# Routing a hybrid layer's last token group inside the mixer, with expert slot tables summed per group

## What is computed

```
mix = hybrid_mixer(x, ...)                      # x @ w_in, mLSTM heads | gated short convolution, @ w_out
x   = layer_norm(ALPHA * x + mix, ln_mix_g, ln_mix_b)              # called x1 here
ffn = grouped_moe(x, router_w, router_b, w_gate, w_up, w_down)
out = layer_norm(ALPHA * x + ffn, ln_moe_g, ln_moe_b)

probs = softmax(xf @ router_w + router_b)       # 16 experts in 4 groups of 4
grp   = argmax(sum of the top 2 of each group)  # one expert group per token
the top 2 experts inside it, gates = their probabilities / their sum
y[token] += gate * (silu(x @ w_gate[e]) * (x @ w_up[e])) @ w_down[e]
```

## Time and profile before

| | |
|---|---|
| median of 3 runs (lowest, highest) | 1700.78 us (1699.57, 1702.06) |
| the profiled execution's own time | 1698.55 us |
| span of its profile | 1696.2 us (2.35 us lie around it) |
| mean granted clock of PE | 0.977 of full speed |
| busy: PE, DVE, ACT, POOL | 1611.2, 1086.9, 659.3, 341.4 us |

### The profile page before, as it was taken

How to read it: one execution, slowest core, us unless ns; L and a number is a source line. 1 busy time by engine, 2 the same in 40 slices (tenths; PEclk the granted TensorE clock), 3 DMA queues, 4 the chain that set the end, 5 groups by cost and what they waited for, 6 DMA issues and landing times. The chain is left out here.

```text
span 1696.2 us, 25177 instructions
## 1 busy us (share of the span) xinstructions
PE 1611.2 (95%) x9494; PEld 1395.9 (82%) x9494; DVE 1086.9 (64%) x1799; ACT 659.3 (39%) x919; POOL 341.4 (20%) x275
## 2 busy tenths in 40 slices
PE   7999999999999999999999279999999999999994
PEld 6888888888888888888888269999999999999993
DVE  3536867557676468665585756565676667666777
ACT  3224424143342343341433324443555455545551
POOL 1100015100052000250000012222333323233333
PEclk9999999999999999999999679999999999999997
DMA  7332336322434225253223626666777777777762
GB/s 238 125 100 75 125 125 215 92 91 92 157 138 162 75 75 184 93 197 100 75 100 125 260 68 206 205 208 202 230 243 244 223 234 251 249 228 234 245 210 95
DMA packets 118922, 279.48 MB, mean 165 GB/s; under 512 B 14688, under 2 KB 16864, under 8 KB 118288
## 3 DMA queue, kind: packets, MB, share of 16 engines
q1 hardware_dynamic: 91536, 188.68, 32.8%
q0 software_dynamic: 26688, 87.05, 17.3%
q10 hardware_dynamic: 576, 2.10, 0.3%
HBM read 232.80 MB, written 48.40 MB: 166 GB/s over the span
## 5 line engine op out<-in xcount | busy, mean ns | idle before, releaser
L1056 PE MATMUL mix_acc<-mix_xT_high,mix_w_high 128*128 128x512 f32 x640 | 256.2, 400 | 2.2 <-DVE mix_w_low L793 2.2
L793 DVE TENSOR_TENSOR mix_w_low<-mix_w_raw,mix_w_high 128x2048 fp32r<-128x2048 f32 x73 | 168.7, 2311 | 138.4 <-ACT mix_w_high L648 138.3
L1058 PE MATMUL mix_acc<-mix_xT_high,mix_w_low 128*128 128x512 f32 x640 | 250.7, 392 | 0.0
L1057 PE MATMUL mix_acc<-mix_xT_low,mix_w_high 128*128 128x512 f32 x640 | 249.9, 390 | 0.0
L648 ACT ACTIVATE mix_w_high<-mix_w_raw 128x2048 fp32r<-128x2048 f32 x73 | 139.8, 1915 | 237.8 <-PE mix_acc L1058 223.9
L1799 DVE TENSOR_TENSOR moe_gate_up_low<-kept_w_gate_up_raw,moe_gate_up_high 128x2048 fp32r<-128x2048 f32 x64 | 146.6, 2291 | 80.4 <-ACT moe_gate_up_high L1669 80.4
L2141 PE MATMUL moe_gate_psum<-moe_xT_high,moe_gate_up_high 128*128 128x288 f32 x512 | 154.1, 301 | 1.4 <-DVE moe_xT_low L1816 1.4
L2143 PE MATMUL moe_up_psum<-moe_xT_high,moe_gate_up_low 128*128 128x288 f32 x512 | 152.0, 297 | 0.0
L2142 PE MATMUL moe_gate_psum<-moe_xT_low,moe_gate_up_high 128*128 128x288 f32 x512 | 151.7, 296 | 0.0
L2142 PE MATMUL moe_up_psum<-moe_xT_low,moe_gate_up_high 128*128 128x288 f32 x512 | 151.6, 296 | 0.0
L2141 PE MATMUL moe_up_psum<-moe_xT_high,moe_gate_up_high 128*128 128x288 f32 x512 | 151.5, 296 | 0.0
(11 more groups left out here) (456 smaller groups left out, 3496.2 us busy)
## 6 DMA issues: line engine op xcount, KB each, us to landing
mix_w_raw<-in_w_in SPq DMA_DIRECT2D x57, 1024.0 KB, 5.3
kept_w_gate_up_raw<-in_w_gate SPq DMA_DIRECT2D x32, 1024.0 KB
kept_w_gate_up_raw<-in_w_up SPq DMA_DIRECT2D x32, 1024.0 KB
kept_w_down_raw<-in_w_down SPq DMA_DIRECT2D x32, 1024.0 KB, 8.6
mix_w_raw<-in_w_out SPq DMA_DIRECT2D x16, 1024.0 KB, 5.1
mix_x_rows<-in_x POOLq DMA_DIRECT2D x16, 512.0 KB, 4.6
kept_conv_or_residual<-in_x POOLq DMA_DIRECT2D x16, 512.0 KB, 5.4
x<-kept_conv_or_residual POOLq DMA_DIRECT2D x12, 512.0 KB, 3.3
```

The costliest lines, as they stand in the source:

```text
L793: dve.tensor_tensor(wl[:, stage % 2], raw[:, stage % 2], wh[:, stage % 2].bitcast(F32), ALU.subtract).then_inc(split_l, 1)
L1056: pe.matmul(out, ah, bh, start=first, stop=False)
L1057: pe.matmul(out, ah, bl, start=False, stop=False)
L1058: return pe.matmul(out, al, bh, start=False, stop=last)
```

## The change

Group 3 is written out too, without the X steps, the load and the split for a next group. In its stage 17 DVE takes, normalises and scales row by row; PE turns row 0 between tiles 2 and 3 and the other rows after the last tile. The rows are turned before the bias is added; the bias's part of the logits is a product of `router_w` with a bias column loaded at the start (`late_b`). SP issues the loads of expert 0 after the last stage's load (their buffers now share room with x's and the queries' and keys' tiles, which are done by then). The block `route` is gone; its constants move to POOL's and DVE's work at the start.

Each routed group's share of the slot table is formed in stages 6 to 8 of the next group (`slot_one_hots`, `slot_sums`, `slots_added`), and that of group 3 at the start of the experts. The table is a sum in SBUF; its one-hots are fp32r, 144 columns of three parts. The number of rounds is worked out after `tables` and loaded at the end of the round. ACT splits three parts of expert 0 ahead; DVE's first split moves behind `tables`. B's result of `down` goes to `pg[1]`, `pu[1]`, so that `down(B)` waits for no reader of A; `gate_up`'s step f = 1 waits for the readers of B instead.

```diff
+def slot_one_hots(dve, keep, w, own, turn, n):
+    N, C = 2 * RT, COLS * N_EXPERTS
+    own.step(dve.tensor_copy(w.rank, keep.pair_rank[:, bass.ds(n * N, N)]))
...
+    own.step(dve.tensor_tensor(w.parts[:, :, 2], keep.icol[:].unsqueeze(1).to_broadcast([P, N, C]),
+                               w.col.unsqueeze(2).to_broadcast([P, N, C]), ALU.is_equal))
+    own.step(dve.tensor_tensor(w.place_oh, keep.i128[:].unsqueeze(1).to_broadcast([P, N, P]),
+                               w.place.unsqueeze(2).to_broadcast([P, N, P]), ALU.is_equal))
+    own.wait(turn)
+    for part, by in ((0, w.token), (1, w.high[:].bitcast(F32))):
+        own.step(dve.tensor_tensor(w.parts[:, :, part], w.parts[:, :, 2].bitcast(F32),
+                                   by.unsqueeze(2).to_broadcast([P, N, C]), ALU.mult))
+    own.wait(turn)
+    dve.tensor_tensor(w.parts[:, :, 2], w.parts[:, :, 2].bitcast(F32), w.low.unsqueeze(2).to_broadcast([P, N, C]),
+                      ALU.mult).then_inc(keep.oh_done, 1)
+
+def slot_sums(pe, keep, w, out):
+    for k in range(2 * RT):
+        ins = pe.matmul(out, w.place_oh[:, k], w.parts[:, k].rearrange("p a b -> p (a b)"), start=(k == 0),
+                        stop=(k == 2 * RT - 1))
+    ins.then_inc(keep.s_ps, 1)
+
+def slots_added(dve, keep, ps, own, turn):
+    own.step(dve.tensor_tensor(slots, slots, ps[:, 0:2 * C], ALU.add))
+    own.wait(turn)
+    dve.tensor_tensor(keep.slots[:, 1], keep.slots[:, 1], ps[:, 2 * C:3 * C], ALU.add).then_inc(keep.s_added, 1)
...
@@ mixer, sync @@
+            sp.dma_start(keep.bias_col[:], column(ln_b), allow_slow_non_contiguous=True).then_inc(consts_in, 16)
...
+            sp.wait_ge(acc_full, (NG - 1) * FULL + OUT0 * NT)
+            load_gate_up(sp, keep, w_gate[0], w_up[0])
...
+            load_down(sp, keep, w_down[0])
+            for t in range(NT):
+                sp.wait_ge(v.x1_ready, (NG - 1) * NT + t + 1)
...
+                sp.dma_start(x1_dram[row:row + P], R[:, t]).then_inc(keep.late_x1, 16)
@@ mixer, scalar, last group @@
+                    for t in range(NT):
+                        one = slice(t, t + 1)
+                        act.wait_ge(lvar_done, g + t + 1)
...
+                        if t == NT - 1:
+                            for half in range(2):
+                                turned_rows(act, v_last, g, 1, half)
+                        act.wait_ge(ln_gained, g * NT + t + 1)
+                        act.activation(R[:, t], R[:, t], ACT.Copy, scale=lrs[:, one]).then_inc(ln_done, 1)
+                        if t == NT - 2:
+                            for half in range(2):
+                                turned_rows(act, v_last, g, 0, half)
+                    logits_taken(act, v_last, g, 0, keep.late_b, False)
+                    turned_rows(act, v_last, g, NT - 1, 0)
+                    logits_taken(act, v_last, g, 1, keep.late_b, False)
+                    exponentials(act, v_last, g)
...
@@ mixer, vector @@
+                        for t in range(NT):
+                            take(g, stage, range(t, t + 1))
...
+                            dve.bn_aggr(lmv[:, t], lstat[:, t]).then_inc(lvar_done, 1)
+                            dve.wait_ge(lvar_done, g + t + 1)
+                            dve.scalar_tensor_tensor(out=R[:, t], in0=R[:, t], scalar=lmv[:, t, 0:1], in1=lng[:],
+                                                     op0=ALU.subtract, op1=ALU.mult).then_inc(ln_gained, 1)
...
+                        for half in range(2):
+                            turned_half(NT - 2, half)
+                        add_bias(0)
+                        turned_half(NT - 1, 1)
+                        add_bias(1)
+                        add_bias(2)
+                        centred_logits(dve, keep, v_last, own, g, g)
+                        add_bias(3)
+                        choices(dve, keep, v_last, own, g, g)
+                        ranks(dve, keep, v_last, own, g, g)
...
                     if routed and stage == 6:
                         ranks(dve, keep, v, own, g, g - 1)
-                        kept_of(dve, keep, v, g - 1)
+                        kept_of(dve, keep, v, own, g, g - 1, dve_idle)
+                        slot_one_hots(dve, keep, w, own, g, g - 1)
+                    if routed and stage == 8:
+                        dve.wait_ge(keep.s_ps, g)
+                        slots_added(dve, keep, aux[0][:, 256:256 + 3 * COLS * N_EXPERTS], own, g)
@@ mixer, tensor @@
-                        if (stage, t) in SLOT:
+                        if (stage, t) in SLOT and not (last and stage > LAST_Y):
                             extra(g, *SLOT[(stage, t)])
+                        if routed and (stage, t) == (7, 0):
+                            pe.wait_ge(keep.oh_done, g)
+                            slot_sums(pe, keep, w, aux[0][:, 256:256 + 3 * COLS * N_EXPERTS])
+                        if last and (stage, t) == (6, 0):
+                            for c in range(KC):
+                                ins = pe.matmul(aux[2][0:TW, 0:1], keep.router_w[:, c], keep.bias_col[:, c:c + 1],
+                                                start=(c == 0), stop=(c == KC - 1))
...
+                        if last and (stage, t) == (ST - 1, NT - 2):
+                            turn_rows(pe, keep, v_last, g, 0, R[:, 0], ln_done)
...
+            turn_rows(pe, keep, v_last, g, 1, R[:, 1], ln_done)
+            turn_rows(pe, keep, v_last, g, 2, R[:, 2], ln_done)
...
+            logits(pe, keep, v_last, 0)
+            turn_rows(pe, keep, v_last, g, 3, R[:, 3], ln_done)
+            fold_logits(pe, keep, v_last, g, 0)
...
+            logits(pe, keep, v_last, 1)
+            fold_logits(pe, keep, v_last, g, 1)
+            counts(pe, keep, v_last, g)
@@ experts @@
+        def trips_wanted(engine, wanted, r):
+            wait_apart(engine, idle, rounds_known, r + 1)
+            engine.reg_mov(wanted, engine.value_load(keep.rounds[0:1, 0:1], min_val=1, max_val=keep.all_rounds))
@@ experts, sync, end of the round @@
+                trips_wanted(sp, wanted, r)
                 all_ended(sp, r)
-                again = n_rounds - 1 - r
+                again = sp.value_load(keep.rounds[0:1, 0:1], min_val=1, max_val=keep.all_rounds) - 1 - r
@@ experts, vector @@
-            dve.wait_ge(keep.late_x1, RT * 16)
-            with dve.Fori(0, n_rounds) as r:
-                one_hots(r)
+            with dve.Fori(0, wanted) as r:
...
+                    slot_one_hots(dve, keep, w, by_group, n, g)
+                    wait_apart(dve, idle, keep.s_ps, n + 1)
+                    slots_added(dve, keep, py[0], by_group, n)
...
+                tables(r)
                 split_gu(r, 0)
-                tables(r)
+                rounds_needed(r)
                 backs(r)
@@ experts, tensor @@
+                if f == 1 and e:
+                    for done in (y_act, y_dve):
+                        pe.wait_ge(done, r * (2 * LAST) + 2 * e)
...
             def down(r, e, k):
-                if k == B:
+                if k == A and e:
                     for done in (y_act, y_dve):
-                        pe.wait_ge(done, r * (2 * LAST) + 2 * e + 1)
...
-                        ins = three(py[q][:], hTh[:, c, AT[k]], hTl[:, c, AT[k]], dh[:, c, s], dl[:, c, s],
+                        ins = three((py, pb)[k][q][:], hTh[:, c, AT[k]], hTl[:, c, AT[k]], dh[:, c, s], dl[:, c, s],
```

More of the change, by code:

```diff
@@ L145, in routing_constants, with turn_rows @@
     own.wait()
-def turn_rows(pe, keep, v, n, t, rows):
-    pe.wait_ge(v.x1_ready, n * RT + t + 1)
+def turn_rows(pe, keep, v, n, t, rows, ready):
+    pe.wait_ge(ready, n * RT + t + 1)
     if t >= 2:
@@ L307, in kept_of @@
+def kept_of(dve, keep, v, own, turn, n, carrier):
     for dst, src in ((keep.rank[:], v.rank), (keep.of_group[:].rearrange("p t g -> p (t g)"), v.of_group),
@@ L436, in mixer @@
         v.banks = ((aux[2], aux[3]), (aux[0], aux[1]))
-        v.shared = True
-        v.logits, v.fold, v.counts = aux[0], aux[1], aux[0]
+        v.logits, v.fold, v.counts = [aux[0][:, 2 * k * P:2 * (k + 1) * P] for k in range(2)], aux[1], aux[0]
         blocks = V[:].rearrange("p c h n -> p (c h) n")
@@ L548, in _, with group @@
             sp.dma_start(keep.router_b[0:N_EXPERTS], router_b.rearrange("(e a) -> e a", a=1)).then_inc(router_in, 16)
-            with sp.Fori(0, NG) as g:
+            def group(g, last):
                 for stage in range(1, ST):
@@ L588, in _, with loads @@
             pool.wait_ge(consts_in, N_CONSTS)
-            def loads(g):
+            def loads(g, last):
                 def load_next(t):
@@ L750, in group @@
                         sigmoid_o(g, SIGMOID_STAGE.index(stage))
-                    if (stage, 0) in SLOT and stage != LAST_Y:
+                    if (stage, 0) in SLOT and stage != LAST_Y and not (last and stage > LAST_Y):
                         extra(g, *SLOT[(stage, 0)], routed)
@@ L757, in group @@
                     for t in range(1, NT):
```

(18 more changed lines are left out.)

577 lines of the change are left out of this document (284 added, 293 removed).

## The result

The changed kernel takes **1686.97 us** (median of 4 runs, 1686.55 to 1687.77) against 1700.32 for the kernel before on the same chip: a ratio of 0.9924, 95% interval [0.9912, 0.9935], 13 us faster. The forecast was 1677, the range 1669 to 1688. The profiled execution has a span of 1685.6 us, 10.6 less than before. The seam and the experts gave what they should; the stretch before the seam grew by 17 us, of which the forecast had 2.7. One execution of a later run (one_pair) took 2319 us at a granted clock of 0.65 and is left out of what follows.

A forecast was written before the change was run, and what follows sets the result against it. PE was taken as the bound, busy in 38 of 40 slices except at the seam and both ends. Terms +0.9 + 1.8 - 21.6 - 6.5 + 1.8 = -23.6 us from 1698.55 gave 1675.0, with 2.2 for the median 1677; range 1669 to 1688.

The forecast's parts named there:

- The seam: From DVE's last take to expert 0's first product: 45.2 us against 66.8, a gain of 21.6 us.
- the experts: Behind the seam: the 15 waits for A's readers go, gaining 6.5 us; bounds nothing and 6.5.
- the table: Seam times from the last take: ranks 21.0, one-hots 27.1, gather's rows 30.2, `same_done` 39.0, expert 0 45.2 us.
- given back at `same_done`: Seam: first transpose waits for DVE's `same_done` until 39.0, gathered rows need until 36.5; 2.5 us of gain lost.
- the slower rival: Experts, step f = 1: PE waits for B's readers in each of 15 experts; 1707 at 2 us each; chance 0.04.
- The end: Behind the last stores: round count loaded by POOL, then SP, two in a row, 1.8 us; bounds nothing and 1.8.
- PE's queue in the mixer: PE's instructions removed and added in the mixer sum to +0.9 us.
- slots: PE in the mixer: three times eight slot products, 1.0 us each time, 3.0 added.
- X steps and row 0's turn: PE in the mixer: four X steps of group 3 removed, 4.1 us; row 0's turn added, 1.0.
- one-hots nothing: DVE in stages 6 to 8: 5.1 us of one-hots fit its idle 5.87 us, so costed at nothing.
- The start: One more column load on SP ahead of stage 1's weights: 1.8 us; bounds nothing and twice 2.63.
- the mixer gives part back: Rival: one-hots at 7.7 us outlast DVE's gap, start and slot products cost more; some 11 us, 1688; chance 0.17.

The follow-up runs named there:

- one_pair: Changed kernel with the experts' row tiles A and B in one pair of PSUM banks again, with the old waits; 1691.59 us, ratio 0.9956.
- same_first: Changed kernel with the instruction that ends `same_done` put right behind the tables, ahead of the moved split and round count; 1683.70 us, ratio 0.9911.
- xt_64: Changed kernel with the mixer's xT 32 bytes lower, at 196544, a multiple of 64; 1674.33 us, ratio 0.9843.
- bias_late: Changed kernel with the bias column's load issued right behind stage 1's weights instead of ahead of them; 1685.02 us, ratio 0.9906.
- left_32: Changed kernel with weights, yT, queries and keys 32 bytes higher and xT left at 196576; 1676.37 us, ratio 0.9856.
- xt_low_32: Changed kernel with xT's high half on a multiple of 64 (196544) and its low half 32 past one; 1683.72 us, ratio 0.9900.

## Why the prediction was right where it was, and wrong

*The direction and the seam were right.* 21.6 us were forecast and 21.5 came (66.8 to 45.3). Every station of the table is within 0.8 us; the closeness of the total has some luck in it, since ranks came 0.8 early and the steps up to the gather's rows took 1.0 longer than forecast. The point that part of the gain is given back at `same_done` held too: the row of the first transpose names DVE's L1993, and same_first moved it.

*The experts were right.* From expert 0's first product to the last product of PE the time fell from 671.2 to 664.3, 6.8 us where 6.5 was the sum of the 15 waits; one_pair brings back 4.6 to 6.1. That 6.8 and 6.5 lie so close is chance in part: the same stretch is 661.0 to 666.0 in the ten traces with the changed kernel's experts, against 671.2 before and 670.3 in one_pair. No wait appeared at f = 1, so the slower rival has no trace behind it.

*The end* was sized at 1.8, two loads of the round count in a row at 0.9 each. From PE's last product to the end of the span are 24.3 us (1661.31 to 1685.6) instead of 23.35, so it cost 0.9. The views of these source lines show the two loads and POOL's last instruction, which ends last (durations in ns, then the start):

```profile
L1572 POOLq TENSOR_LOAD <-kept_rounds x1: 510/510/510, 1680.5 to 1680.5; - x1
...
L1608 SPq TENSOR_LOAD <-kept_rounds x1: 278/278/278, 1681.6 to 1681.6; - x1
...
L1480 POOLq DRAIN  x1: 3528/3528/3528, 1681.8 to 1681.8; - x1
```

POOL's load and the register work behind it stand in the way of that drain; SP's load runs beside it and costs nothing. So the price of one load was right, and that both would count was wrong. The Trainium skill (DMA: Bandwidth & Descriptors, Latency and other measured facts) gives such a load a floor of some 600 ns. In this trace five of six take less, 0.28 to 0.51 us, and one 0.80. So the floor isn't borne out here, and the estimate of 1.2 for two loads has the same fault as my 1.8.

*PE's queue in the mixer* was right in the items it had: slots 3.0 of 3.0, bias 0.7 of 1.0, X steps and row 0's turn -3.1 of -3.1, one-hots nothing. **The step that failed is its sum, "+0.9"**: it counted instructions added and removed and took the duration of the 3,456 that stay from the old trace. 2,688 of them became 5.6 ns slower, some 14 us by the stages and 13 to 14 by xt_64, because a tile that the change only moves was laid 32 bytes off the others.

*The start* was sized at 1.8 and measured 3.5 in these two traces. bias_late and the landings put the column at some 2.6; the rest is that the trace of before had an early landing, which I took as fixed. In the eight traces with the changed kernel's queue PE's wait ranges from 5.1 to 7.3 us, so 3.5 is itself one draw. The term also rested on a range of 0.99 to 2.63 us for such loads, where the old trace goes down to 0.51.

*The sum.* With the start at 3.5, PE's queue at 0.6, the loss at xT of 14.1, the passages at -1.5, the seam at -21.5, the experts at -6.8 and the end at 0.9, the terms add up to -10.7; the span fell by 10.6. Around the span lie 1.55 us instead of 2.35, which I did not follow up.

*The rival "the mixer gives part back"* had 1688 us, near the result, but by another mechanism: its one-hots outlast nothing, and the slot products cost what I had said. That the range held the time is luck: it reached that far only for this rival's sake. (The page before has 36 slices of 40 at nine tenths or more, not 38 as the prediction says; the four others are the holes that it names.) Without the place of xT the forecast would have stood 3 us above xt_64's 1674.3.

## What to carry to other kernels

When a change moves a buffer that a matrix product reads, look up where the product's operands start, modulo 64 bytes, relative to one another; in the profile the sign is a larger distance of start times with no wait listed and the clock unchanged. Keep the tiles that alternate in one stream of 512-column products on the same remainder, and lay a tile from the far end of the memory behind a pad if need be. And when a load is moved ahead of small ones, ask which wait the consumer stands behind: moving the load gave nothing until its split was moved ahead of the wait for the constants.

## What was unexpected in the hardware

In the mixer, a stream of fp32r products of 512 columns runs at 0.2277 us a product when all its tiles start at the same remainder of 64 bytes, at 0.2316 when xT is 16 off and at 0.2332 when it is 32 off, whether xT streams or is held. In the experts, with the operands 32 off, products of 512 columns went from 0.2299 to 0.2333 and those of 288 columns from 0.1328 to 0.1333. Whether the common remainder is 0 or 32 doesn't matter (left_32). The Trainium skill (SBUF — State Buffer, Who interferes with whom) gives TensorE two independent read ports, one for the operand that streams and one for the weight load. No run here shows ports; what the runs show is that products that wait for no other engine still lose 5.5 ns each by the places of their tiles. The Trainium skill (SBUF — State Buffer, Operand start alignment) says which starts are allowed, and that this is about legality and not speed. These runs are about speed alone. Why even those products of a triple are slower whose own operands agree (xt_low_32) was not settled.
